# Two transformer blocks on one core: expert stage in one piece, shorter steps between units, norms applied as token factors, second block reordered

## The reference

```python
# first block
x = x + ga * merge_heads(diff_attend(...), mla_attend(...))
h = modulate(rmsnorm(x), sf, scf)
x = x + gf * moe(h)              # 32 experts, each token goes to 4
x = rmsnorm(x)
# moe: for each expert e over its tokens
hid = xb @ w1[e] + b1[e]         # 1024 -> 2048
y = clamped_swiglu(hid[:, :1024], hid[:, 1024:]) @ w2[e] + b2[e]
# second block
xn = rmsnorm(x); proj = xn @ w_in
merged = sum(sigmoid(xn @ w_gate[b]) * (y_b @ w_branch[b]) for b in (pool, dilated, stick, s5))
x = x + merged @ w_out
hn = rmsnorm(x); gu = hn @ w_up
x = x + (silu(gu[:, :F]) * gu[:, F:]) @ w_down
out = rmsnorm(x)
```

## Time and profile before

| | |
|---|---|
| runs shown (3) | 1990.1, 1993.76, 1995.72 us; median 1993.76 |
| profiled execution | 1995.57 us, its span 1993.7 us |
| TensorE busy | 1752.5 us (88%), 8422 records |
| VectorE, ScalarE, GpSimd busy | 440.4, 280.8, 114.5 us |
| mean granted TensorE clock | 0.939 |
| memory traffic | 547 MB, 274 GB/s over the span |
| chain that ended last | TensorE 73%, transfers 15%, SyncE's queue 5%, VectorE 3%, ScalarE 2% |

### The profile page before, as it was taken

How to read it: one execution, slowest core, us unless ns; L and a number is a source line. 1 busy time by engine, 2 the same in 40 slices (tenths; PEclk the granted TensorE clock), 3 DMA queues, 4 the chain that set the end, 5 groups by cost and what they waited for, 6 DMA issues and landing times.

```text
span 1993.7 us, 20775 instructions
## 1 busy us (share of the span) xinstructions
PE 1752.5 (88%) x8422; PEld 1053.4 (53%) x8422; DVE 440.4 (22%) x1011; ACT 280.8 (14%) x569; POOL 114.5 (6%) x258
## 2 busy tenths in 40 slices
PE   6999999597998787868799959699998999899997
PEld 3535675142343233424244414277776788688885
DVE  2135221011111111112011201232456622211101
ACT  4023321011011010001001101012222210100000
POOL 1000000000000000000046600000020000000000
PEclk9999999797999898989899969799998999999999
DMA  9225356999998999889999999963434325344340
GB/s 378 104 87 220 132 203 237 420 419 414 417 417 371 419 415 412 329 337 418 410 419 416 417 420 419 410 249 117 152 132 143 119 71 190 125 151 169 113 161 21
DMA packets 135845, 547.01 MB, mean 274 GB/s; under 512 B 10109, under 2 KB 23549, under 8 KB 99774
## 3 DMA queue, kind: packets, MB, share of 16 engines
q1 hardware_dynamic: 129200, 529.83, 67.0%
q0 software_dynamic: 3200, 11.01, 1.5%
q10 hardware_dynamic: 3342, 4.77, 0.7%
HBM read 537.97 MB, written 7.60 MB: 274 GB/s over the span
## 4 chain that ended last, share of the span: by engine, by line
PE 73%; DMA 15%; SPq 5%; DVE 3%; ACT 2%; issue 1%; ACTq 0%; DVEq 0%
PE PS L1138 15%; DMA ring<-in_w 7%; PE PS L1154 7%; DMA arena<-in_w 6%; SPq L1623 5%; PE PS L2151 4%; PE PS L2161 4%; PE PS L2153 4%; PE PS L1995 3%; PE PS L2016 3%; PE PS L2008 3%; PE PS L1134 3%; PE PS L1166 3%; PE PS L1108 3%; PE PS L497 2%
## 5 line engine op out<-in xcount | busy, mean ns | idle before, releaser
L1138 PE MATMUL PS<-ring,arena 128*32 128x512 f32 (+2 forms) x1272 | 320.8, 674 | 67.2 <-DMA ring<-in_w 33.7
L1138 PE MATMUL PS<-arena 128*32 128x512 f32 (+2 forms) x776 | 222.0, 666 | 25.4 <-DMA ring<-in_w 20.8
L1138 PEld LDWEIGHTS PS<-ring,arena 128*32 128x32 f32 (+2 forms) x1272 | 100.0, 141 | 242.6 <-issue 242.6
L1154 PE MATMUL PS<-ring,arena 128*32 128x512 f32 (+2 forms) x600 | 155.2, 733 | 34.5 <-DMA ring<-in_w 21.8
L1154 PE MATMUL PS<-arena 128*32 128x512 f32 (+2 forms) x424 | 132.9, 732 | 34.9 <-DMA ring<-in_w 20.0
L1425 DVE TENSOR_SCALAR arena<-PS 128x512 f32<-128x512 f32 x28 | 19.2, 687 | 537.0 <-PE PS L1138 537.0
L1138 PEld LDWEIGHTS PS<-arena 128*32 128x32 f32 (+2 forms) x776 | 68.7, 143 | 126.3 <-issue 126.2
L1154 PEld LDWEIGHTS PS<-ring,arena 128*32 128x32 f32 (+2 forms) x600 | 46.4, 148 | 113.1 <-issue 112.1
L1154 PEld LDWEIGHTS PS<-arena 128*32 128x32 f32 (+2 forms) x424 | 41.0, 156 | 108.5 <-issue 107.5
L2151 PE MATMUL PS<-arena,ring 128*128 128x256 f32 x352 | 82.7, 390 | 6.6 <-DVE arena L2290 6.6
L1995 PE MATMUL PS<-arena,ring 128*128 128x256 f32 x384 | 84.6, 380 | 0.0
(11 more groups left out here) (430 smaller groups left out, 2043.2 us busy)
## 6 DMA issues: line engine op xcount, KB each, us to landing
ring<-in_w SPq DMA_DIRECT2D x234, 1024.0 KB, 18.6
arena<-in_w SPq DMA_DIRECT2D x150, 1024.0 KB, 18.9
ring<-in_w_ada SPq DMA_DIRECT2D x24, 1024.0 KB, 7.6
ring<-in_w_in SPq DMA_DIRECT2D x22, 1024.0 KB, 13.6
ring<-in_w_up SPq DMA_DIRECT2D x20, 1024.0 KB, 9.6
ring<-in_w_gate SPq DMA_DIRECT2D x16, 1024.0 KB, 6.7
ring<-in_w_down SPq DMA_DIRECT2D x11, 1024.0 KB, 7.0
ring<-in_w_out SPq DMA_DIRECT2D x8, 1024.0 KB, 4.9
```

The lines of the kernel that those rows point to most:

```text
L1138: m = pe.matmul(bank(("up", i, b))[rows[n], :], xs[:, k, rows[n]], tiles[n][:, b * 512:(b + 1) * 512], start=False, stop=k == 7, skip_grou ...
L1154: m = pe.matmul(bank(("down", i, c))[rows[n], :], actT[:, k, rows[n]], tiles[n][:, a:a + 512], start=k == 0, stop=k == 7, skip_group_check ...
```

## The change

- The experts run as one list (MAIN_STEPS); the branch around MORE stands behind it and ahead of the second block, on all five engines.
- `flip` of unit i-1 moves behind step k = 1 of up i; b1 moves from ahead of the up products to behind the last one; `b2` moves behind unit 1's gates. A scatter waits for each half of its input by itself. In the last unit VectorE copies both halves.
- Recurrence: s5body is split into s5scan 0, s5scan 1 and s5turn, one per part of the list; POST is interleaved anew, with gelu behind the last s5out.
- stick: ScalarE does Exp and Ln for two heads together, at the odd head.
- dil: the maximum is negated in the same instruction; instead of scaling the rows, VectorE scales a 128x128 identity by 1/sum, and TensorE's transposes become products with it. This VectorE work moves from the first step of a unit to its second; a unit's first step stands ahead of the last two of the unit before.
- The norm ahead of ff: sums of squares are taken between the x2 products, with one output column; ff 0 and ff 1 run on x times the weight only, and their results are multiplied by the token factor, which is formed beside them; ff 2 and later use hn.
- The last norm: additions, squares and sums follow each bank of the down product as it ends; the factor is formed for two columns and spread by a product; VectorE and GpSimd share the last multiplication; the output leaves in four transfers.

```diff
             for i in range(lo, hi):
                 for k in range(8):
                     yield ("up", i, k)
+                    if k == 1 and i > lo:
+                        yield ("flip", i - 1)
...
                 if i < last:
                     yield ("gather", i + 1)
                     yield ("gates", i + 1)
+                if i == lo + 1 and sort[8]:
+                    yield ("b2",)
                 if i > lo:
                     yield ("scatter", i - 1)
-                elif sort[8]:
-                    yield ("b2",)
-                yield ("flip", i)
...
-        CUT, LAST = 7, len(MAIN_UNITS) - 1
+        LAST = len(MAIN_UNITS) - 1
...
+                    if k == 7:
                         w.wait_ge(b1_zero, 3)
...
-                                pe.matmul(bank(("up", i, b))[rows[n], :], one.to_broadcast([128, width]), b1t[:, b * 512:(b + 1) * 512], start=True, stop=False, skip_group_check=True)
+                                m = pe.matmul(bank(("up", i, b))[rows[n], :], one.to_broadcast([128, width]), b1t[:, b * 512:(b + 1) * 512], start=False, stop=True, skip_group_check=True)
```

```diff
+            units = [(hs, t) for hs in range(4) for t in range(2)]
+            for n in range(len(units) + 1):
+                if n < len(units):
...
+                    yield first + [("dil", hs, t, 0)]
+                if n:
+                    yield [("dil",) + units[n - 1] + (1,)]
+                    yield [("dil",) + units[n - 1] + (2,)]
...
+                    yield left + [("s5body", q, hp), ("s5scan", q, hp, 0)]
+                    yield [("s5scan", q, hp, 1)]
+                    yield [("s5turn", q, hp)]
                     left = [("s5out", q, hp)]
...
+            yield left + [("gelu",)]
...
+        POST += [("s5init",), ("bias_of", 0), ("bias_of", 1)]
         put(rec)
+        early = [("sq", 2816, 4), ("sk", 3328, 4)]
+        early = [list(projT_steps(*v)) for v in early] + [list(projV_steps("sv", 3840, 512)), list(projT_steps("pu", 0, 4))]
+        early += [list(projT_steps("lq", 512, 6)), list(projT_steps("lk", 1280, 6)), list(projV_steps("lv", 2048, 768))]
+        early = [part for v in early for part in v]
+        late = list(gate_steps(2)) + [[("poolprod",)]] + [[("branch", 0, f)] for f in range(8)] + list(gate_steps(1))
+        last = [[("glu", f)] for f in range(4)] + [[("kept", 0, j)] for j in range(0, 8, 2)] + [[("branch", 3, f)] for f in range(8)]
+        for n, part in enumerate(early):
+            POST += part
...
+            put(rec)
+            if n >= 6:
+                put(att)
+        for n, part in enumerate(late + last):
+            POST += part
+            if n % 2:
+                put(rec)
             put(att)
...
+        POST += [("x2", 0)]
+        for f in range(1, 8):
+            POST += [("x2", f), ("x2sum", f - 1)]
```

```diff
-                                i = pe.transpose(psum(s + (a,), b * 128, (b + 1) * 128), x[:, (a + b) * 128:(a + b + 1) * 128], ident)
+                                i = pe.matmul(psum(s + (a,), b * 128, (b + 1) * 128), x[:, (a + b) * 128:(a + b + 1) * 128], dil_d[DILS.index((hs, t)) % 2], start=True, stop=True, skip_group_check=True)
...
+                        if h % 2:
+                            pair = [wide[wide_of["stick", n] % 2][:, 384:768] for n in (h - 1, h)]
+                            own.wait()
+                            for v in pair:
+                                own.count(act.activation(v, v, ACT.Exp, scale=-1.0))
+                            own.wait()
+                            for v in pair:
+                                act.activation(v, v, ACT.Ln, bias=1.0).then_inc(stick_z, 1)
...
+            for f in range(22):
+                room(G["ff", f])
+                for k in range(8):
+                    if f == 0 and k == 7:
+                        x2_sum(7)
+                    up(f, k, 0)
...
+                if f == 0:
+                    w.wait_ge(ff_root, 4)
+                    room(G["x2factor",])
+                    for t in range(2):
+                        i = pe.matmul(psum(("x2factor",), t * 128, (t + 1) * 128), ones, ffd[t], start=True, stop=True, skip_group_check=True)
...
+            for i, (mine, more_of) in enumerate(((2, 0), (4, 0), (5, 1), (5, 3))):
+                w.wait_ge(out_ready, mine)
+                if more_of:
+                    w.wait_ge(out_more, more_of)
+                sp.dma_start(to[:, 2 * i:2 * i + 2, :], xv[:, 2 * i:2 * i + 2, :]).then_inc(out_done, 16)
```

377 lines of the change are left out of this document (230 added, 147 removed).

## The result

The changed kernel takes 1971.65 us (median of 4 runs, 1969.7 to 1973.0), the kernel before, beside it on the same chip, 1994.74 (4 runs): a ratio of 0.988 with a 95% interval of 0.987 to 0.990, 23 us less. Forecast were 37 less, 1957. The range of 1938 to 1974 holds the result, 2 us from its upper end; about 0.6 of the forecast gain came.

What follows compares the result with a forecast made beforehand. Memory traffic was taken to bound the experts, TensorE the second block. Experts -35, entrance +6, mixers +14, norm -12 and tail -10 sum to -37, from the median 1993.8 to 1957 us; range 1938 to 1974.

Steps and rivals of the forecast that it cites:

- D: Rival, whole kernel: parts do as forecast, but mixers at their upper bound and branch at +9; 1970 us; chance 0.11.
- unit 4: Experts: flip 4 and b1 of unit 5 leave the stretch ahead of unit 5; 5.5 of 5.9 us won.
- the split: Experts, cut at unit 7: without the cut and its empty pipeline, unit 8 begins earlier; 19.5 of 20.4 us won.
- B: Rival, experts: ring still fills at single units, only the start and half the split won; -20, 1972 us; chance 0.14.
- C: Rival, experts: b1 behind the last product holds each unit's last slots 3.7 us longer; 52 more, 2009 us; chance 0.04.
- E: Rival, entrance: branch is free because TensorE's queue is further ahead, no gap before first us; 1951 us; chance 0.08.
- (a): Mixers: s5body 0's second half waits for us 3's bank, freed after VectorE's eight operations on x; 3.1 us.
- (b): Mixers: paired Exp and Ln delay VectorE's even-head step and the turn behind it, so s5out waits 3.5, twice: 7 us.
- (c): Mixers, gate (2,5): a scan piece stands ahead of the diagonal that dil (0,1)'s transposes need; 3.8 us.
- (e): Mixers, behind s5out (3,1): gelu stands ahead of dil (1,1)'s diagonal in VectorE's queue; 6.4 us.
- (d): Mixers: TensorE stalls at poolprod, which stands behind dil (1,1); 2.5 us.
- Rival A: Mixers: half of the new stalls and of their slow clock are hidden; 16 less, 1941 us; chance 0.20.

Runs made afterwards that it cites:

- the two other kernels: Kernel before with only the flips, b1, b2 and scatter waits: 1976.31 us; kernel before with the whole expert part: 1969.1 us.
- a later order: Changed kernel with heads unpaired, attention ahead of recurrence throughout the list's second half, us 3 taken up before rescaling x: 1945.2 us.
- the last two kernels: Changed kernel, heads unpaired, us 3 earlier, attention first at two parts: 1938.67 us; that plus transposes and last multiplication on VectorE alone: 1930.89 us.

## Why the prediction was right, and where it was wrong

The range holds the result, but near its end: 22.5 us came of 37 forecast, and D, with the mixers at their bound, was nearer than my own sum.

**Experts, right, in mechanism and size.** -35 forecast, -34.8 measured; in the eleven profiles with the whole expert part this stretch takes 990.2 to 993.0, so -33 to -36. The parts hold too. Without the single list 16.1 came, for 10 at the start, 5.5 at unit 4 and up to 4.4 at the split. With the start's and unit 4's gains taken off and the 1.7 of the later start added, my times for units 1, 5 and 8 (328, 620.4 - 3.5, 835.5) are 329.7, 608.6 and 821.7; measured are 329.5, 609.3 and 822.2. Rivals B (-20) and C are out, by the two kernels that have the expert part alone.

**Entrance, the mechanism right, the size within its scatter.** The step was "+3.4, and after such a rest TensorE runs at 1.2 GHz for a while: +2 to 3". In the profile of the changed kernel the idle time grew by 3.4, to the tenth, but that is in part luck: in four of ten profiles the branch was 1.4 longer. The slow clock cost 4.7, because it lasted beyond the 16 records from which I took the 2: the 32 records of us 0 and us 1 took 10.21 instead of 7.14, and further on the 16 of us 2 took 6.59 instead of 5.39. Over the ten profiles the two together come to 3.4 to 9.5; the 6 lies inside. The Trainium skill's 108 ns for a compare-and-branch (Advanced Engine Details and Errata, Control Flow Timing), which would have given E's time, is contradicted again for TensorE by the 6266 ns and by what the kernel without a branch gained. ScalarE's and VectorE's own records of the branch are 50 and 72 ns.

**Mixers, the mechanism right and the size wrong: +22.2 for +14.** The five waits over 2 us stood where (a), (b), (c) and (e) had them, with their causes, and removing the causes removed the waits. By the table, +22.2 is +6.9 idle, +9.6 lost to the clock and +5.7 work; forecast were 22.8 - 18.6 = +4.2, 10 - 4 = +6 and +4.
- Idle: of the two waits in (b) one came out 2.7 longer than 3.5, with GpSimd beside the turn (3.48 without it), the other 1.3 shorter. (a) was 2.3 for 3.1, (c) 4.3 for 3.8, (e) 6.4 for 6.4. (d), poolprod, was 0.9 for 2.5; four waits of 0.3 to 1.3, 3.0 in all, were missed. That the sum came within 2.6 is partly errors that cancel.
- The clock is the step that failed most: "behind five of them at 2 us". It was 2.7 for each of the five. Removing two gaps gave 2.9 each; removing 20.2 us of idle gave back 13.4.
- Work: the transposes are 4.0 of 5.7. The other 1.7 stayed open; no run has them alone.

Rival A (half of the stalls hidden) is out: the idle time came out longer than the sum, not half of it. D had the mixers at +24 and the branch at +9, nearer to what came than my own sum. (The bound of +24 does not follow from "half as much again": half of the 22.8 more is +25, half of the 33 more is +30.)

**Norm ahead of the feed-forward, the mechanism right.** No wait stands ahead of ff 0 or ff 2. -12.2 came for -12, but both are counted from the one profile of before; from the 193.8 of the two other kernels with that stretch unchanged it is -10.2. No run has this part alone.

**Tail, 2.4 short.** "Five products of 0.42 on VectorE beside three on GpSimd" was the failed step: beside GpSimd they took 0.69. That is 1.3 of the 2.4. Another 0.75 lies in the end, 3.75 from VectorE's last operation to the end of the span instead of 3, and 0.4 in the chain up to the multiplication. One us of it came back with VectorE alone.

## What to carry to other kernels

Walk each in-order queue through a new order and write down, for every product of the bound engine, which operations stand ahead of its input: all five stalls over 2 us were foreseen so, and two more (4.62 and 2.03) came with a later order for which that walk was left out. Three small edits (attention steps ahead at two places, one bank taken up earlier, one pairing undone) gave some 33 us, more than the whole change had. Count a gap on TensorE not at its length alone but with the slow clock behind it. How much that is varies: here 13.4 us came back with 20.2 of idle, but the kernel before lost 3.8 with 18.5 idle, and waits up to 1.7 us in the last two kernels cost nothing. Two steps joined to save table loads (41 on ScalarE in the changed kernel, 45 with the heads unpaired) make everything behind the first one wait for the second; check what stands there.

## What the runs showed of the hardware

- VectorE and GpSimd slow each other when VectorE takes two operands from SBUF: its 128x512 multiplications took 1.1 to 1.4 instead of 0.68 us (one of them 2.26 beside a GpSimd operation of 1.89), GpSimd's 128x256 ones 1.05 instead of 0.72, its small copies 0.5 to 0.65 instead of 0.19, and a final product of 0.41 took 0.69. For the tail, giving GpSimd three of eight products made the whole slower than VectorE alone. The Trainium skill (SBUF — State Buffer, SBUF: two separate sides) says that a VectorE operation with two SBUF inputs and a GpSimd operation that reads SBUF shut each other out for a whole instruction; the traces agree in kind. I had not weighed it.
- The branch on TensorE's queue took 6.16 us at the split and, at the entrance, 6.2 to 6.3 us in six profiles and 7.6 to 7.8 in four. Behind the one at the entrance ScalarE loads a table twice more, 1.28 us each. On VectorE the record of the branch is only 0.07 us, but at the split its next instruction starts 5.5 us behind it (5.6 in the kernel with the flips and b1 alone) with nothing in the profile that it waited for, and SyncE's next stands 5.1 to 5.3 behind its own branch in every kernel that has one. At the split of the kernel before that pause of VectorE, and not TensorE's branch, was in the chain of waits:

```profile
799.11 0.07 DVEq L2592
799.18 5.48 issue
```

- Behind a gap of 6.17 us TensorE's granted clock was 0.50 from 1390 to 1396 and 0.68 in the 6 us after. Windows of the changed kernel at four of its gaps (columns as in the first windows above; the clock is the last column but two):

```profile
1390.00:1396.00 6.00, 5.44 (x21) 3.17 (x22) 3.41 (x7) 0.00 (x0) 3.27 (x4) 0.50 0.01 3
1396.00:1402.00 6.00, 6.00 (x22) 5.02 (x22) 5.76 (x14) 0.52 (x1) 0.00 (x0) 0.68 0.00 0
1448.00:1454.00 6.00, 6.00 (x23) 3.61 (x20) 2.84 (x8) 0.00 (x0) 0.00 (x0) 0.50 0.00 0
1504.00:1510.00 6.00, 4.43 (x19) 4.15 (x20) 1.44 (x4) 0.98 (x2) 0.00 (x0) 0.72 0.00 0
1546.00:1552.00 6.00, 3.11 (x13) 3.06 (x14) 1.68 (x4) 1.68 (x3) 0.00 (x0) 0.55 0.01 3
```

The gap of 2.24 (ahead of 1447.6) brought over 6 us at 0.50, the one of 6.17 over 9, the longest, 6.41, under 5 (from 1548.9 to 1553.4, then 1.00 again): what is lost behind a gap does not follow its length. Nor is it the same for the same gap: behind the 4.32 the clock was at 0.50 for 3.5 us in the changed kernel and for 6.0 in the one with the heads unpaired.
